# Latent attention with the softmax division moved onto the probabilities and the value product turned round

## The reference, cut to what matters

```python
def one_block(args):                       # 4 query blocks of 128
    qi, bi = args
    sc = jnp.einsum('bqhd,bkhd->bhqk', qi, k) * scale
    mask = key_chunk[None, :] <= q_chunk[:, None]
    p = jax.nn.softmax(jnp.where(mask, sc, -jnp.inf), axis=-1)
    return jnp.einsum('bhqk,bkhd->bqhd', p, v)
...
return o.reshape(b, s, MLA_HEADS * MLA_V) @ w_o
```

## Time and profile before

| what | value |
|---|---|
| median of 3 runs | 1933.32 us (1933.29 to 1933.35) |
| the profiled execution | 1933.38 us |
| its span, first to last instruction | 1931.6 us |
| PE busy in the span | 1916.9 us (99%) |
| attention stage, 866.9 to 1016.9 us: PE, ACT, DVE busy | 148.30, 102.98 and 93.39 of 150 us |
| granted TensorE clock | 1.00 |

### The profile page before, as it was taken

The page is one execution under the profiler, slowest core; times in us unless marked ns, Lnnn a source line. Parts: engine busy times, 40 slices in busy tenths (PEclk is TensorE's granted clock), DMA queues, the critical chain, the costliest instruction groups (busy, mean ns, idle before and its releaser), DMA issues.

```text
span 1931.6 us, 23515 instructions
## 1 busy us (share of the span) xinstructions
PE 1916.9 (99%) x9586; PEld 1630.2 (84%) x9586; DVE 1218.8 (63%) x1673; ACT 947.4 (49%) x1343; POOL 50.1 (3%) x83
## 2 busy tenths in 40 slices
PE   8999999999999999999999999999999999999999
PEld 7889998888888888898889888888888889888887
DVE  5645553345768676877745868667634357776867
ACT  5333334234645445568744644535564646353543
POOL 1000000000000000010000000000000000000000
PEclk9999999999999999999999999999999999999999
DMA  7233322322341431311014143241232223414141
GB/s 249 77 99 94 92 72 93 109 98 88 109 144 35 150 119 59 100 59 46 23 44 131 44 153 103 72 153 44 88 110 75 79 66 109 136 61 152 34 141 68
DMA packets 163398, 182.47 MB, mean 94 GB/s; under 512 B 7682, under 2 KB 125015, under 8 KB 163163
## 3 DMA queue, kind: packets, MB, share of 16 engines
q1 hardware_dynamic: 160746, 176.67, 28.4%
q0 software_dynamic: 2528, 4.29, 0.8%
q10 hardware_dynamic: 16, 0.00, 0.0%
HBM read 175.62 MB, written 2.11 MB: 92 GB/s over the span
## 4 chain that ended last, share of the span: by engine, by line
PE 96%; DVE 2%; ACT 1%; DMA 1%; issue 0%; POOL 0%; ACTq 0%
PE psum L96 29%; PE psum L98 29%; PE psum L97 29%; PE psum L2261 2%; PE psum L2239 2%; PE psum L565 1%; PE psum L2692 1%; PE psum L2249 1%; DVE weights_lo L413 1%; PE psum L2217 1%; PE psum L2675 0%; PE psum L1012 0%; PE psum L983 0%; PE psum L1004 0%; PE psum L993 0%; PE psum L981 0%
## 5 line engine op out<-in xcount | busy, mean ns | idle before, releaser
L96 PE MATMUL psum<-norm_T_hi,weights_hi 128*128 128x512 f32 (+1 forms) x1440 | 538.9, 374 | 0.2 <-DVE weights_lo L413 0.2
L98 PE MATMUL psum<-norm_T_hi,weights_lo 128*128 128x512 f32 (+1 forms) x1440 | 534.2, 371 | 0.0
L97 PE MATMUL psum<-norm_T_lo,weights_hi 128*128 128x512 f32 (+1 forms) x1440 | 533.9, 371 | 0.0
L413 DVE TENSOR_TENSOR weights_lo<-raw_weights,weights_hi 128x2048 fp32r<-128x2048 f32 (+3 forms) x136 | 299.2, 2200 | 225.9 <-ACT weights_hi L407 225.9
L407 ACT ACTIVATE weights_hi<-raw_weights 128x2048 fp32r<-128x2048 f32 (+3 forms) x136 | 249.4, 1834 | 189.7 <-PE psum L98 189.7
L98 PEld LDWEIGHTS psum<-norm_T_hi,weights_lo 128*128 128x128 f32 x1440 | 271.4, 188 | 46.5
L96 PEld LDWEIGHTS psum<-norm_T_hi,weights_hi 128*128 128x128 f32 x1440 | 271.5, 189 | 45.7 <-DVE weights_lo L413 0.5
L97 PEld LDWEIGHTS psum<-norm_T_lo,weights_hi 128*128 128x128 f32 x1440 | 271.6, 189 | 45.3
L96 PE MATMUL psum<-weights_hi,act_T_hi 128*128 128x512 f32 (+1 forms) x528 | 204.3, 387 | 0.0
L98 PE MATMUL psum<-weights_hi,act_T_lo 128*128 128x512 f32 (+1 forms) x528 | 203.2, 385 | 0.0
L97 PE MATMUL psum<-weights_lo,act_T_hi 128*128 128x512 f32 (+1 forms) x528 | 203.0, 385 | 0.0
(11 more groups left out here) (318 smaller groups left out, 2480.6 us busy)
## 6 DMA issues: line engine op xcount, KB each, us to landing
raw_weights<-in_ffn_w_dram SPq DMA_DIRECT2D x32, 1024.0 KB, 5.5
scratch<-in_ffn_w_dram SPq DMA_DIRECT2D x32, 1024.0 KB, 5.5
raw_weights<-in_w_in_dram SPq DMA_DIRECT2D x26, 512.0 KB, 5.3
raw_weights<-in_w_in_dram SPq DMA_DIRECT2D x11, 1024.0 KB, 5.3
raw_weights<-in_w_up_dram SPq DMA_DIRECT2D x8, 1024.0 KB, 6.6
scratch<-in_w_up_dram SPq DMA_DIRECT2D x8, 1024.0 KB, 6.6
raw_weights<-in_w_down_dram SPq DMA_DIRECT2D x8, 1024.0 KB, 5.3
scratch<-in_w_down_dram SPq DMA_DIRECT2D x8, 1024.0 KB, 5.2
```

Source lines behind the costliest of these rows:

```text
L96: pe.matmul(out, ah, bh, start=start, stop=False, skip_group_check=more)
L97: pe.matmul(out, ah, bl, start=False, stop=False, skip_group_check=more)
L98: return pe.matmul(out, al, bh, start=False, stop=stop, skip_group_check=more)
L413: dve.tensor_tensor(WL[:, u % 2, 0:c], raw(units[u].slot)[:, 0:c], WH[:, u % 2, 0:c].bitcast(F32), SUB).then_inc(w_lo, 1)
```

## The change

The division moves ahead of the transposes. The exponentials also sum their rows (`accum_out`), and a new DVE function `scaled(n)` inverts the sums and multiplies the probabilities in `SB`, in place, in two steps: query block 3 when its exponential is done, the other three when all are. `turn` now waits for `probs_scaled` in place of `probs_ready`.

The value product is turned round. V (128 by 64) stands and the turned probabilities move: five fp32 matmuls of 384, 384, 256, 128 and 128 columns. `PT` is laid out by key block, query block and query for it. The outputs come with the 64 value columns on the partitions, an even head in the lower half of bank 6 and an odd one in the upper half, which is the layout the output product wants: `normed`, the column of ones, `ON` and the `out` transposes go. `pair_hi` on ACT and `out_lo` on DVE read bank 6 directly. So `values(n)` of an even head waits until both have read the pair before it, and every `values(n)` waits ahead of its first matmul for all three copies of `PT`.

```diff
 def turn(n, c):
-    pe.wait_ge(pex.sem, pex.at(4 * n + RAISED[c]))
+    pe.wait_ge(psc.sem, psc.at(4 * n + RAISED[c]))
...
 def values(n):
-    if n:
-        pe.wait_ge(ond.sem, ond.at(n))
-    for t in ORDER:
-        if t == 2:
-            pe.wait_ge(a1.sem, a1.at(n + 1))
-        elif t != 0:
-            pe.wait_ge(pte.sem, pte.at(2 * n + (1 if t == 3 else 2)))
-        for j in range(t + 1):
-            mm = pe.matmul(PS[:, 6, t * MV1:t * MV1 + MV1], PT[:, off[t] + j * P:off[t] + j * P + P],
-                           VN[:, n // 4 % 2, j, n % 4, :], start=j == 0, stop=j == t)
-    mm.then_inc(pvd.sem, 1)
+
+    pe.wait_ge(pte.sem, pte.at(2 * n + 2))
+    pe.wait_ge(a1.sem, a1.at(n + 1))
+    if n % 2 == 0 and n:
+        pe.wait_ge(paired.sem, paired.at(n // 2))
+        pe.wait_ge(tl.sem, tl.at(n // 2))
+    row = n % 2 * MV
+    for j in range(NT):
+        t = max(j, 1)
+        pe.matmul(PS[row:row + MV, OUT, t * P:S], VN[:, n // 4 % 2, j, n % 4, :], PT[:, j, t:NT, :],
+                  start=j == 0, stop=True, skip_group_check=j > 0)
+    pe.matmul(PS[row:row + MV, OUT, 0:P], VN[:, n // 4 % 2, 0, n % 4, :], PT[:, 3, 2, :],
+              start=True, stop=True).then_inc(pvd.sem, 1)
...
 turn(n, 2)
-for what in before:
-    job(what)
 values(n)
```

On ACT, `pair_hi` stands at the head of the even heads' list, before the copy of chunk 0, and the exponentials carry the sum:

```diff
+def pair_hi(pair):
+    act.wait_ge(pvd.sem, pvd.at(2 * pair + 2))
+    act.activation(by_residue(NTH[:, pair, :]), in_order(PS[:, OUT, :]), ACT.Copy).then_inc(paired.sem, 1)
...
-                   bias=nms[:, n % 2, t:t + 1], scale=qs[:, n // 4 % 2, t, n % 4:n % 4 + 1]).then_inc(pex.sem, 1)
+                   bias=nms[:, n % 2, t:t + 1], scale=qs[:, n // 4 % 2, t, n % 4:n % 4 + 1],
+                   accum_out=den[:, n % 2, t:t + 1]).then_inc(pex.sem, 1)
...
+if n % 2 == 0 and n:
+    pair_hi(n // 2 - 1)
 for c in (0, 2):
```

On DVE:

```diff
+def scaled(n):
+
+    for c, ts in enumerate((slice(3, 4), slice(0, 3))):
+        dve.wait_ge(pex.sem, pex.at(4 * n + (1, 4)[c]))
+        dve.reciprocal(rden[:, n % 2, ts], den[:, n % 2, ts]).then_inc(rcp.sem, 1)
+        dve.wait_ge(rcp.sem, rcp.at(2 * n + c + 1))
+        for t in (ORDER[:1], ORDER[1:])[c]:
+            z = SB[:, off[t]:off[t] + (t + 1) * P]
+            dve.tensor_scalar(z, z, rden[:, n % 2, t:t + 1], None, MUL).then_inc(psc.sem, 1)
...
 def out_lo(pair):
-    m = idx[("out", pair)]
-    dve.wait_ge(ev.sem, ev.at(emptied[m]))
-    dve.tensor_tensor(by_residue(NTL[:, pair, :]), in_order(PS[:, bank(m), :]),
+    dve.wait_ge(paired.sem, paired.at(pair + 1))
+    dve.tensor_tensor(by_residue(NTL[:, pair, :]), in_order(PS[:, OUT, :]),
...
-    normed(n)
+    if n + 1 < MH:
+        scaled(n + 1)
```

More of the change, by code:

```diff
@@ L2174, in mla @@
                 e += 2 if job[0] == "kv" else 1
-                x += 1 if job[0] in ("tr", "out") else 0
+                x += 1 if job[0] == "tr" else 0
                 emptied.append(e)
@@ L2217, in job @@
                             mm = pe.transpose(PS[0:MQK, bank(m), t * P:t * P + P], QK[:, h // 4 % 2, j, t, h % 4, :], IDENT[:, :])
[L2218 to L2222, removed]
                         mm.then_inc(tp.sem, 1)
@@ L2270, in _ @@
                 for n in range(MH):
-                    behind, between, before, gemms = jobs_at(n)
+                    behind, between, gemms = jobs_at(n)
                     if n + 1 == MH:
@@ L2290, in last_turn @@
                         turn(MH - 1, c)
-                tail.extend((last_turn, lambda: values(MH - 1), lambda: job(("out", MH // 2 - 1))))
+                tail.extend((last_turn, lambda: values(MH - 1)))
             @block.scalar
@@ L2308, in empty @@
                         act.activation(VN[:, g % 2, t, :, 0:MV], kv[:, :, MNOPE:MNOPE + MV], ACT.Copy).then_inc(ev.sem, 1)
-                    elif what[0] == "out":
-                        act.wait_ge(tp.sem, tp.at(turned[m]))
-                        act.activation(by_residue(NTH[:, what[1], :]), in_order(src), ACT.Copy).then_inc(ev.sem, 1)
                     else:
@@ L2381, in _ @@
                             act.wait_ge(pvd.sem, pvd.at(n))
-                        w = len(CHUNKS[c]) * P
-                        act.activation(PT[:, 4 * c * P:4 * c * P + w], PS[:, 3, 0:w], ACT.Copy).then_inc(pte.sem, 1)
-                    for what in between + before:
+                        t, w = (3, None, 1)[c], len(CHUNKS[c])
+                        act.activation(PT[:, 0:w, t, :], PS[:, 3, 0:w * P].rearrange("p (j q) -> p j q", j=w), ACT.Copy).then_inc(pte.sem, 1)
+                    for what in between:
                         empty(what)
@@ L2393, in _ @@
                         squares(g + 1, 0)
-                empty(("out", MH // 2 - 1))
+                pair_hi(MH // 2 - 1)
             @block.gpsimd
@@ L2505, in _ @@
                 masks(0)
+                scaled(0)
                 for n in range(MH):
@@ L2535, in mla @@
             tl.passed(8); ropes.passed(16); tp.passed(turned[-1]); ev.passed(emptied[-1])
[L2536 removed]
+            for s in (smk, sc, pex, psc):
                 s.passed(4 * MH)
@@ L2978, in build @@
             compressed = mla_down(block, after, came, dn, up)
-            tail, made, freed, (spare, taken) = mla(block, compressed, dn)
-            banks = ((0, 1, 2, spare), (3, 4, 6, taken))
+            tail, made, freed, taken = mla(block, compressed, dn)
+            banks = ((0, 1, 2, 5), (3, 4, 7, taken))
             up, dn, turn = bank_sets(banks)
```

47 lines of the change are left out of this document (16 added, 31 removed).

## The result

| | before | after |
|---|---|---|
| median of the runs | 1933.34 us | 1964.16 us (4 runs, 1960.98 to 1964.40) |
| ratio | | 1.0157, 95% interval 1.0144 to 1.0169 |
| span of the profiled execution | 1931.6 us | 1962.6 us (run of 1964.38) |
| PE busy / not busy in it | 1916.9 / 14.7 us | 1925.5 / 37.1 us |
| granted clock of TensorE, mean | 1.00 | 0.996 |

The change makes the kernel 30.8 us slower. 21.2 were forecast, and 1964.16 lies 2.2 us above the range. The sign was right and so were the waits; a loss of clock that the sum did not have came on top.

What follows compares the result with a forecast made beforehand. PE's chain, 96% of the page, was taken to bound the kernel. PE's work -3.8, waits +5.7 and +15.8, heads 0, 1 and 10 +1.9, +1.1, +2.3, vanished waits -1.8: +21.2 on 1933.4 gives 1954.6 us, range 1948 to 1962.

Steps and rivals of the forecast that it cites:

- PE's work, -3.8: Value products at 2.16 for 2.18 us give -0.3, and the dropped output transposes -3.5 us.
- The waits, +25.0 (21.2 + 3.8): All terms but PE's own work: +5.7, +15.8, +1.9, +1.1, +2.3, and -1.8 us for old waits that vanish.
- Plain heads: Product waits for ACT's last chunk copy, 0.42 plus 0.29 restart, 0.71 us in eight heads (0, 1, 3, 5 ... 13): +5.7 us.
- Even heads: Product waits for `out_lo`, behind copy and three masks on DVE, 2.25 us in seven heads (2 to 14): +15.8 us.
- Head 0: Nothing ahead covers its scaling; second chunk waits for all four exponentials, an inversion and two scalings: +1.9 us.
- Head 1: DVE runs without a gap, so scaling makes the copy of chunk 1 late beyond the 0.71: +1.1 us.
- Head 10: Late exponentials, scaling and the keys' normalisation make a wait near 4.6 us, 2.3 more than an even head's: +2.3 us.
- the signs that the prediction gave: Product waits for ACT's copy (odd heads), `out_lo` (even); PE busy falls 3 to 4 us; over 2.3 us a product means error.
- the clock falls in the waits: Rival, 5%: each of seven even heads' waits sets off a half-clock fall, 7 x 2.3 = 16 us more: 1970.7 us.
- Scaling: About 1.6 us a head on DVE, exponentials 0.6 us later on ACT; covered by PE's work except in heads 0, 1, 10.
- Hidden waits (1927.8 and 1943.8): Rivals at the start of `values`: all waits hidden, -5.6 us, 1927.8, 3%; only `out_lo` hidden, +10.4 us, 1943.8, 4%.
- the dearer product (1969.6): Rival, 6%: weights loads show in the turned product's ten passes, costing some 3.1 us each; total +36, 1969.6 us.

Runs made afterwards that it cites:

- experiment 9: Kernel of experiment 1 with each of the 16 value products issued twice in a row, the second behind no wait: 1976.59 us.
- experiment 1: Changed kernel with DVE's `out_lo` moved from behind the three masks to the head of the even heads' list: 1946.73 us.
- experiment 7: Kernel of experiment 1 without row sums, inversions and scaling, so the outputs are not divided: 1942.74 us.
- experiment 6: Kernel of experiment 1 with the key's four transposes put between the last transposes of the probabilities and the value product: 1943.86 us.
- Experiments 1 and 2: Experiment 1 has its own line; the second is the changed kernel with 16 unused identity transposes before each even head's product, from head 2: 1956.51 us.
- experiment 5: Kernel of experiment 1 with the product's matmuls reordered, a 128-column one first and a long 384-column one last: 1945.88 us.
- experiment 4: Kernel before the change with only the row sums and the scaling of the probabilities ahead of the transposes added: 1945.65 us.
- experiments 10 to 12: Changed kernel with head n+2's scores ahead of head n's product: 1965.75 us; also keys' rotation later: 1967.49; scores ahead with key transposed and emptied earlier: 1963.34.
- experiment 10: Changed kernel with head n+2's scores before head n's product, ACT emptying the key before chunk 2, `out_lo` before DVE's chunk 1 copy: 1965.75 us.

## Why the prediction was right in kind and too low

**What bounds the kernel.** Right. PE's chain is the time; ACT and DVE have at least as much idle time as before, and it did not help.

**PE's work, -3.8: 0.0 in the busy rows.** Its own parts hold: 2.16 us for a product at pace (experiment 9), and the transposes are gone (-3.5). What is missing is in two things. The start-up behind a wait is booked as busy: 0.21 x 15 = 3.2 us, less the 0.7 that the waits of before, now gone, had in heads 5, 9 and 10 (0.24, 0.26 and 0.22). The prediction had this in its waits (0.24 of its 0.29). And what stands behind the new product takes 0.14 longer than behind the old one: 16 x 0.14 = 2.2. -3.8 + 3.2 - 0.7 + 2.2 = +0.9, measured 0.0 in experiment 1, where the clock is whole; 0.9 us is not accounted for. Only the 0.14 was left out of the sum. Where it comes from stays open.

**The waits, +25.0 (21.2 + 3.8): 22.4 of standing still plus 2.5 of start-up, 24.9.** Right in all, with errors that cancel, so the closeness is in part luck. Plain heads: 0.46 + 0.21 = 0.67 for 0.71. Even heads: 15.3 / 7 + 0.21 = 2.40 for 2.25. Head 0: 1.6 for 1.9 (the prediction's own terms, 874.5 + 0.15 - 872.65, make 2.0). Head 1: 1.4 - 0.46 = 0.9 for 1.1. Head 10 has 1.8 at a place of its own for 2.3. The cause of each was the one named: `out_lo` moved (experiment 1) takes 10.0 of standing still away, and what is left at the product is mostly ACT's copy, with or without scaling (experiment 7). Of the signs that the prediction gave, the owners of the waits and the chain came as said; PE's busy time rose where it was to fall by 3 to 4 us, and the product took 2.37 in a plain head, over the 2.3 that was to be a sign of error: 0.21 of that is the start-up.

**What was not tried.** The wait of the plain heads also comes from where the waits stand: all of them ahead of the product's first matmul. By the layout of `PT` the matmuls of the last two key blocks (128 and 256 columns) and the single block of 128 need chunks 0 and 1 only. At the pace of experiment 9 these 512 of 1280 columns are about 0.86 us of work (an estimate, 2.16 x 512 / 1280), more than the 0.46 for which PE waits for chunk 2. DVE's copy of chunk 1 may then be the one waited for, as in experiment 6. No run puts them first with the wait behind them, so no run shows what that would give, or whether the sums in bank 6 allow that order.

**The clock: the step that failed.** The sum had no term for it; "the clock falls in the waits" was a rival at 5% and 16 us, 2.3 for each of seven heads, and against it stood that "PE is at work before and after each wait". The runs show 8.6 us: five falls at 1.65. Work on both sides did not keep the clock up. With 8.6 added to 21.2 the sum is 29.8, against 30.8 measured. The rival's own size was off in the other direction: it had all seven waits set off a fall and 0.6 us more for each. Experiments 1 and 2 show it from two sides, by taking the wait away and by filling it. What told heads 2 and 8 from the other five stays open: in head 10 the same two waits left the clock whole in experiment 1's trace and not in experiment 5's, so the length of the waits alone does not decide. The Trainium skill (TensorE: Matmul & The Clock Gate, Part 1, HAM oscillation) says that a matmul stream broken by long enough waits falls back to the half clock and pays for it again and again. The traces agree on that kind of loss, with five falls behind seven waits of 2.2 us on average; the waits in the page's own example are longer than these, so it did not say that these are long enough.

**Scaling.** The prediction called it covered but for three heads. Under the new order that is near (4.0 us, experiment 7). In the old order it costs 12.5 (experiment 4), of which 6.9 are waits: whether it is covered depends on the order around it.

**The other rivals.** Hidden waits (1927.8 and 1943.8) and the dearer product (1969.6) did not come. 1943.8 was the forecast's price for a covered `out_lo`; the kernel that has it takes 1946.73.

## What to carry to other kernels

When a product is turned so that its first matmul needs a piece of an operand that only its last ones needed before, the copies that used to lie under the product come to stand in front of it, in every pass of the loop; look for what is issued between the last producer and the first consumer before counting saved matmuls. An instruction that the product newly waits for must be moved ahead of unrelated work in its engine's list: here one line was worth 17 us of 31, nearly half of it clock. A wait of some 2 us on TensorE in each turn of a loop is to be priced with the matmuls behind it at the lower clock for a while, here 1.65 us on a wait of 2.2, in five heads of seven; and moving other work over a wait helps only if that work's own operands are earlier than the ones it covers (experiments 10 to 12).

## What the runs showed of the hardware that was not expected

- The clock fell behind waits of some 2.2 us in a stream that is otherwise nearly full, and not behind all of them. It also fell behind pairs of shorter ones: 1.15 and 1.13 us (experiment 5), 0.84 and 0.64 (experiment 10). One run of four of the kernel after took 1960.98 us rather than 1964, with a mean clock of 0.997 for 0.996.
- A value product that follows a wait shows 0.21 us more busy time than one that does not (2.37 and 2.16), so a busy sum hides part of a wait's price.
- The same scores take 2.16 us behind projections and 2.35 behind the new product (experiment 9), and a projection behind it takes 0.14 us more as well; neither the order nor the shapes of the product's matmuls changed that.
- The accumulator reads on ACT take 0.19 us each but start 0.09 before their activation ends, so a head's exponentials grew from 2.29 to 2.67 us; the next activation in head 9 starts at 976.96:

```profile
976.14 0.81 ACT L2328 ACTIVATE scratch<-scratch,small 128x512 f32<-128x512 f32 x1
976.86 0.19 ACT L2328 ACTIVATION_READ_ACCUMULATOR scratch<-scratch,small 128x1 f32 x1
```
